# Modulation with its weight blocks stationary, in a two-layer trunk step on one core

## The chip, the cores and the metric

The kernel runs on one core of one Trainium2 chip. The metric is device time in microseconds of one execution. Three runs of the kernel before are shown; their median is the time before.

## What is computed

Two layers of a diffusion trunk, for 512 latent tokens and 128 context tokens of width 1024, all in fp32. Every layer is:

```
m = silu(c) @ w_mod[L] + b_mod[L]        # 6 vectors of 1024: shift, scale, gate, twice
h = rms_norm(x) * scale + shift          # latent tokens take c, context tokens c_ctx
x = x + gate * mixer(h)                  # layer 0: chunk gating + grouped attention; layer 1: MLA + short conv
h = rms_norm(x) * scale2 + shift2
logits = h @ w_router; aff = softmax(logits over the 16 experts)
gate, idx = top_k(aff, capacity)         # 64 latent and 16 context tokens for each expert
y[idx] += gate * (silu(h[idx] @ w_gate) * (h[idx] @ w_up)) @ w_down
x = x + gate2 * y
```

w_mod is 2 x 1024 x 6144 fp32, 48 MB. It is used for two vectors alone, c and c_ctx.

## The kernel before

**Streams.** All large weights (w_mod, the projections, 16 experts of 6 MB a layer) come in pieces of 1 MB through four `stage` slots, 128 partitions x 2048. SyncE (SP) issues them in the order of `plan_weights`; a piece is issued once the slot's last reader is done (`load`, L612 on, for the experts `expert_piece`, L629 on). Projection and expert weights are split in two parts: ScalarE (ACT) copies the high one into one of three w_hi slots (L1355, L1635), VectorE (DVE) subtracts for the low one (w_lo, L1740), and TensorE (PE) makes three passes. All of PE's products are issued in helper L800, its transposes at their own lines.

**Order of the work.** Each engine's program is written out by hand. Layer: norm sums on PE (`arena,cst`, a matrix of constants), root and scaling on DVE and ACT, projections, attention, output projection, norm sums again, then the eight tiles of h with the router's products (`logits`, 48 products with `router_hi`/`router_lo`), softmax, transposes of the affinities (L1216), transposes of h (L1224, 40 of them) which ACT copies out and sends to `h_dram`, the top-k on DVE (L2091 to L2098), the gates' transposes on PE (L1243, L1244), their copies by ACT into `gates` and `slots` (L1644 to L1649). With the slots there, GpSimd (POOL) gathers each expert's 80 rows from `h_dram` by an indirect transfer (L766), four ahead; PE transposes them (L1258), and at an expert's end POOL adds the rows to `acc_dram` by an indirect transfer (L775). At the start of layer 1 the sum is read back (`arena<-acc_dram`).

**The modulation.** It is 24 chunks of 512 columns of w_mod, 12 for each layer, two pieces of 1 MB for each chunk. The table `MOD_AT` (L98) says at which named place of the program each chunk lies, and the PSUM plan (`PsumPlan`, L109 on), the weight stream and all engines follow it. For a chunk (`mod_rows`, L865) silu(c) and silu(c_ctx) are the stationary operand, padded to 32 columns (`sP`), and w_mod moves:

```
ins = mm(bank(("mod rows", c))[32 * k:32 * k + 32, :], sP[:, 4 * half + k, :], w[:, k, :], half == 0, half == 1)
```

Eight such products of 512 columns leave the result as rows, in four strips of a bank. ACT copies the bank to `mrow` (L1342), PE turns it with four transposes (`turn_mod`, L873, L877), and DVE adds the four strips (L1826), adds the bias (L1829) and for two chunks of a layer makes `amul` (L1834). `sel` (a selection matrix) later shares `mrow`'s space.

Of the kernel before, what the change touches and what calls it, by code (L numbers as in the profile page):

```python
# [28 lines left out]
P = 128  # L29
D = 1024  # L30
# [62 lines left out]
def turned_banks(i):  # L93
# [4 lines left out]
MOD_AT = {"start": [0, 1, 2, 3], "qk": [4, 5], "first scores": [6, 7], (0, "out"): [8, 9], (0, "norm"): [], (0, "apply"): [10, 11], (0, "soft"): [],  # L98
          (0, "top"): [12, 13, 14], "acc": [15, 16], "next norm": [17], "cq": [18, 19], (1, "out"): [20, 21], (1, "norm"): [],
          (1, "apply"): [22, 23], (1, "soft"): [], (1, "top"): []}  # L100
# [6 lines left out]
class PsumPlan:  # L107
# [21 lines left out]
    def one(self, name, reader, banks=1):  # L129

        b = self.ring % 8
        if banks == 2:
            b = (b + b % 2) % 8
        self.add(name, list(range(b, b + banks)), reader)
        self.ring = b + banks
# [13 lines left out]
def plan_psum():  # L149
# [3 lines left out]
    def mod(at):  # L153

        chunks = MOD_AT[at]
        for n, c in enumerate(chunks):
            one(("mod rows", c), "act")
            if n:
                one(("mod turned", c - 1), "dve")
        if chunks:  # L160
            one(("mod turned", chunks[-1]), "dve")
# [5 lines left out]
    for c in MOD_AT["start"]:  # L167
        one(("mod rows", c), "act")
        if c == 2:
            one(("mod turned", 1), "dve")  # L170
        elif c:
            one(("mod turned", c - 1), "dve")
        if c == 1:
            one((0, "norm", 0), "dve", 2)
    one(("mod turned", MOD_AT["start"][-1]), "dve")
    for L in range(LAYERS):
# [51 lines left out]
        for n in range(len(STEPS) + LAG[L] + 1):  # L228
            if n < len(STEPS):
                p.add((L, "S", n), [0, 1, 2, 3], "act")  # L230
            if L == 0 and 1 <= n <= len(MOD_AT["first scores"]):
                p.add(("mod turned", MOD_AT["first scores"][n - 1]), [2 * n + 3], "dve")
            if L == 0 and n < len(MOD_AT["first scores"]):
                p.add(("mod rows", MOD_AT["first scores"][n]), [2 * n + 4], "act")
# [6 lines left out]
        for m in range(KD):  # L241
            p.add((L, "out", m), [2 * (m % 3), 2 * (m % 3) + 1], "dve")
        p.add((L, "norm", 1), [6, 7], "dve")
        p.ring = 0
        mod((L, "out")), mod((L, "norm")), mod((L, "apply"))
        one((L, "logits"), "act", 2)
        one((L, "logits turned"), "dve")
        mod((L, "soft"))
        one((L, "aff"), "act"), one((L, "aff ctx"), "act")
        for t in range(NT):  # L250
            one((L, "h", t), "act", 2)
        if L == LAYERS - 1:
            one("gate rows", "act")
            for t in range(NT):
                one(("x out", t), "act", 2)
        mod((L, "top"))
# [1975 lines left out]
```

## Time and profile before

| | before |
|---|---|
| median of 3 runs | 1506.52 us (1504.7 to 1508.73) |
| profiled execution | 1508.51 us, of which the span of its instructions is 1506.6 |
| PE busy | 1275.3 us (85%) |
| DVE busy | 888.4 us (59%) |
| ACT busy | 736.9 us (49%) |
| POOL busy | 226.8 us (15%) |
| granted clock of PE, mean | 0.924 of 2.4 GHz |
| moved | 323.19 MB, 215 GB/s over the span |

Times in the trace count from the span's start. The experts of layer 0 run from about 421 to 733, those of layer 1 from about 1163 to 1480. "PEld" is PE's weight load, which can overlap the product before it. An fp32 product appears as two records.

### The profile page before, as it was taken

The page shows a single profiled execution, that of the slowest core. Times are in us where ns is not written, and L with a number is a line of the kernel's source. Part 1 is how long each engine was busy: PE and PEld are TensorE (multiplying, and loading weights), DVE is VectorE, ACT ScalarE, POOL GpSimd, SP SyncE. Part 2 cuts the span into 40 slices and gives each one's busy share as a digit, 9 for nine tenths or more (in the row PEclk, how much of TensorE's full clock was granted, in tenths as well). Part 3 has the DMA queues.
Part 4 walks back from the last instruction along what each step waited for, and adds up shares of the span by engine and source line. Part 5 has one row for each costly group of instructions (what it writes and reads, how often), then busy time and mean ns, then how long its engine had stood idle before and what let it go on. Part 6 is the DMA issues. An engine that isn't in the chain of part 4 may idle for free.

```text
span 1506.6 us, 18070 instructions
## 1 busy us (share of the span) xinstructions
PE 1275.3 (85%) x7500; PEld 921.2 (61%) x7500; DVE 888.4 (59%) x989; ACT 736.9 (49%) x867; POOL 226.8 (15%) x129
## 2 busy tenths in 40 slices
PE   5899968997489988989659998999964999998991
PEld 3779736893256555556449984668933655555560
DVE  3612476325758778878374252553156878887883
ACT  2512247414447777767253114553144765666662
POOL 3000010020102222211050000000101023333230
PEclk9889889997689999999789998899976999999996
DMA  9702071006779999999872320003058799999985
GB/s 342 220 29 84 28 279 47 1 29 223 292 242 344 359 355 355 364 357 360 270 216 85 98 87 28 1 2 112 1 223 290 279 355 322 357 360 338 358 321 166
DMA packets 99047, 323.19 MB, mean 215 GB/s; under 512 B 6367, under 2 KB 30142, under 8 KB 82582
## 3 DMA queue, kind: packets, MB, share of 16 engines
q1 hardware_dynamic: 87360, 283.54, 52.3%
q0 software_dynamic: 9152, 30.53, 8.0%
q10 hardware_dynamic: 2454, 7.96, 1.4%
q8 instruction: 60, 0.98, 0.3%
q14 instruction: 21, 0.17, 0.0%
HBM read 298.20 MB, written 23.81 MB: 214 GB/s over the span
## 4 chain that ended last, share of the span: by engine, by line
PE 45%; DMA 23%; DVE 15%; ACT 13%; issue 3%; POOL 1%; ACTq 0%; SPq 0%; DVEq 0%; POOLq 0%
PE psum L800 42%; DMA stage<-in_moe_w_up 9%; DVE w_lo L1740 8%; ACT w_hi L1635 5%; DMA stage<-in_moe_w_gate 4%; ACT arena L1562 3%; DMA stage<-in_moe_w_down 2%; DMA stage<-in_w_mod 2%; DMA acc_dram<-arena 2%; DVE arena L2010 2%; DMA arena<-h_dram,arena 1%; ACT arena L1342 1%; POOL arena L684 1%; DMA arena<-acc_dram 1%; DVE h_lo L1740 1%
## 5 line engine op out<-in xcount | busy, mean ns | idle before, releaser
L1740 DVE TENSOR_TENSOR w_lo<-stage,w_hi 128x2048 fp32r<-128x2048 f32 (+1 forms) x216 | 490.4, 2280 | 222.1 <-ACT w_hi L1635 123.7
L1635 ACT ACTIVATE w_hi<-stage 128x2048 fp32r<-128x2048 f32 x192 | 366.6, 1914 | 154.9 <-DMA stage<-in_moe_w_up 49.4
L800 PE MATMUL psum<-w_hi,h_hi 128*80 128x512 f32 (+1 forms) x848 | 333.6, 393 | 55.0 <-DVE w_lo L1740 39.6
L800 PE MATMUL psum<-w_lo,h_hi 128*80 128x512 f32 (+1 forms) x848 | 328.1, 387 | 0.0
L800 PE MATMUL psum<-w_hi,h_lo 128*80 128x512 f32 (+1 forms) x848 | 327.5, 386 | 0.0
L800 PE MATMUL psum<-h_hi,w_hi 128*128 128x320 f32 x672 | 211.3, 314 | 4.7 <-DVE h_lo L1784 4.7
L800 PEld LDWEIGHTS psum<-w_hi,h_hi 128*80 128x80 f32 (+1 forms) x848 | 130.9, 154 | 136.7 <-DVE w_lo L1740 42.3
L800 PE MATMUL psum<-h_lo,w_hi 128*128 128x320 f32 x672 | 209.8, 312 | 0.0
L800 PE MATMUL psum<-h_hi,w_lo 128*128 128x320 f32 x672 | 209.6, 312 | 0.0
L775 POOL DMA_INDIRECT acc_dram<-arena x32 | 101.1, 3160 | 482.4 <-ACT arena L1673 252.7
L800 PEld LDWEIGHTS psum<-w_hi,h_lo 128*80 128x80 f32 (+1 forms) x848 | 131.1, 155 | 64.4 <-issue 2.5
L800 PEld LDWEIGHTS psum<-w_lo,h_hi 128*80 128x80 f32 (+1 forms) x848 | 131.3, 155 | 53.8 <-issue 1.9
L800 PE MATMUL psum<-arena 128*64 128x128 f32 (+8 forms) x940 | 132.5, 388 | 24.4 <-ACT arena L1562 10.2
L1342 ACT ACTIVATE arena<-psum 128x256 f32<-128x256 f32 (+7 forms) x133 | 75.3, 615 | 137.1 <-PE psum L800 120.0
L800 PEld LDWEIGHTS psum<-h_hi,w_hi 128*128 128x128 f32 x672 | 128.2, 191 | 6.4 <-issue 6.4
L800 PEld LDWEIGHTS psum<-h_lo,w_hi 128*128 128x128 f32 x672 | 128.2, 191 | 0.2 <-issue 0.2
L800 PEld LDWEIGHTS psum<-h_hi,w_lo 128*128 128x128 f32 x672 | 128.1, 191 | 0.0
L800 PEld LDWEIGHTS psum<-arena 128*64 128x64 f32 (+4 forms) x940 | 78.0, 175 | 81.1 <-issue 55.7
L1562 ACT ACTIVATE arena<-psum,arena 128x640 f32<-128x640 f32 x64 | 50.3, 790 | 63.8 <-DVE arena L2010 63.8
L684 POOL TENSOR_TENSOR arena<-arena 128x640 f32<-128x640 f32 x24 | 39.0, 1626 | 272.7 <-ACT arena L1365 271.2
L1355 ACT ACTIVATE w_hi<-stage 128x2048 fp32r<-128x2048 f32 x22 | 41.9, 1910 | 66.9 <-PE psum L800 63.4
L1365 ACT ACTIVATE arena<-xT 128x640 f32<-128x640 f32 x32 | 23.1, 735 | 100.7 <-DVE xT L2068 73.1
(225 smaller groups left out, 1200.5 us busy)
## 6 DMA issues: line engine op xcount, KB each, us to landing
stage<-in_moe_w_gate SPq DMA_DIRECT2D x64, 1024.0 KB, 8.5
stage<-in_moe_w_up SPq DMA_DIRECT2D x64, 1024.0 KB, 8.9
stage<-in_moe_w_down SPq DMA_DIRECT2D x64, 1024.0 KB, 7.3
stage<-in_w_mod SPq DMA_DIRECT2D x48, 1024.0 KB, 7.8
stage<-in_ev_w_in SPq DMA_DIRECT2D x7, 1024.0 KB, 10.8
stage<-in_od_w_in SPq DMA_DIRECT2D x7, 1024.0 KB, 10.0
h_dram<-arena ACTq DMA_DIRECT2D x10, 512.0 KB, 3.4
stage<-in_ev_w_out SPq DMA_DIRECT2D x4, 1024.0 KB, 5.4
```

The lines of the kernel that those rows point to most:

```text
L684: nc.gpsimd.tensor_tensor(rstd, rstd, sq[k % 2], ALU.add).then_inc(sq_added, 1)
L775: pool.indirect_dma_start(acc_dram[L], bass.IndirectOffsetOnAxis(slots[:, e:e + 1], 0), ysb[e % 2], None, compute_op=ALU.add).then_inc(sca ...
L800: return pe.matmul(o, w, x, start=first, stop=last, skip_group_check=True)
L1342: freeing(nc.scalar.activation(dst, src, ACT.Copy, **kw))
L1355: nc.scalar.activation(split_slot(w_hi, pc["q"], pc["n"]), slot(pc), ACT.Copy).then_inc(hi_ready, 1)
L1365: nc.scalar.activation(rstd if k == 0 else sq[k % 2], xT[:, k, :], ACT.Square).then_inc(sq_ready, 1)
L1562: ins = nc.scalar.activation(p[:, LKEYS * a:LKEYS * a + LKEYS], src[:, 0:LKEYS], ACT.Exp, bias=largest(i, a), accum_out=total(i, a))
L1635: nc.scalar.activation(split_slot(w_hi, q0), stage[:, PIECE * (p0 % SLOTS):PIECE * (p0 % SLOTS) + PIECE], ACT.Copy)\
L1740: return nc.vector.tensor_tensor(dst, src, hi.bitcast(F32), ALU.subtract)
L2010: ins = nc.vector.tensor_reduce(largest(i, a), src[:, 0:LKEYS], AX.X, ALU.max, negate=True)
```

## The change

The weight block becomes the stationary operand. A chunk is 32 products: 128x128 of w_mod stationary, the two columns of `sT` (silu(c), silu(c_ctx)) moving. The result falls out with features on partitions, so `sP`, `mrow`, the ACT copy, the transposes and the DVE reduction go; DVE adds the bias from the bank (`turned_mod`). A chunk can be issued in eight parts (`mod_part`).

The chunks' places change. (0, out), (0, apply) and (0, top) with 2, 2 and 3 chunks become: 8 ahead of the norm sums ("sum"), 9 and 10 behind them ("root"), 11 in eight parts among the logits' products, 12 ahead of the transposes of h ("rank"), 13 between the context's gates and the latent gates ("top"), and 14 moves to the end of the layer ("acc"). In layer 1: 20 ahead of the norm sums, 21 and 22 behind, 23 among the logits. DVE takes up the results at these places, some of them before the top-k and some behind the slots.

Around the top-k: DVE, not ACT, copies the latent gates and slots out, right behind the top-k; ACT first copies the context's, then splits g0, g1 and u0 of expert 0; DVE splits the first gathered rows ahead of u0. SP holds the fifth expert piece until the first gather has landed. POOL issues the gate rows' transfers behind the first four gathers, and `final_norm` goes to `cs`, issued earlier. The banks of the PSUM plan around it are fixed by number.

```diff
...
-          (1, "apply"): [22, 23], (1, "soft"): [], (1, "top"): []}
+MOD_AT = {"start": [0, 1, 2, 3], "qk": [4, 5], "first scores": [6, 7], (0, "sum"): [8], (0, "root"): [9, 10], (0, "logits"): [11],
+          (0, "rank"): [12], (0, "top"): [13], "acc": [14, 15, 16], "next norm": [17], "cq": [18, 19], (1, "sum"): [20],
+          (1, "root"): [21, 22], (1, "logits"): [23], (1, "rank"): [], (1, "top"): []}
...
                     else:
+                        if m == SLOTS:
+                            sp.wait_ge(gathered[0], 16 * (E // AHEAD * L + 1))
                         sp.wait_ge(lo_ready, m + (moe_q[L] - SLOTS + 1))
...
+            def mod_part(c, i):
+
+                name, (half, k) = ("mod", c), divmod(i, 4)
+                pc = piece[("mod", c, half)]
+                if i == 0:
+                    begin(name)
+                if k == 0:
                     pe.wait_ge(stage_in[pc["p"] % SLOTS], arrived(pc["p"]))
-                    for k in range(4):
-                        ins = mm(bank(("mod rows", c))[32 * k:32 * k + 32, :], sP[:, 4 * half + k, :], w[:, k, :], half == 0, half == 1)
+                w = slot(pc).rearrange("p (k n) -> p k n", k=4)
+                for b in range(MODC // P):
+                    ins = mm(bank(name)[:, 2 * b:2 * b + 2], w[:, k, P * b:P * b + P], sT[:, i, :], i == 0 and b == 0, i == KD - 1)
+                if k == 3:
                     ins.then_inc(psum_full if half else mod_used, 1)
...
-            for c in MOD_AT["start"]:
-                mod_rows(c)
-                if c:
-                    turn_mod(c - 1)
-                if c == 1:
-                    norm_sum_of_two((0, "norm", 0))
-            turn_mod(MOD_AT["start"][-1])
+            modulation("start", slice(0, 2))
+            norm_sum_of_two((0, "norm", 0))
+            modulation("start", slice(2, None))
...
+                modulation((L, "sum"))
                 norm_sum_of_two((L, "norm", 1))
-                modulation((L, "out"))
-                modulation((L, "norm"))
-                modulation((L, "apply"))
+                modulation((L, "root"))
...
                 for k in range(KD):
+                    for c in MOD_AT[(L, "logits")]:
+                        mod_part(c, k)
                     h_tile(h0 + KD + k + 1)
...
-                for what in ("g0", "g1", "u0")[:2 + L]:
-                    expert_split(0, what)
...
-                filled(act, (L, "gates"))
-                src = bank((L, "gates"))[0:CAP_L, :]
-                nc.scalar.activation(gates[0:CAP_L, :], src[:, 0:E], ACT.Copy)
-                freeing(nc.scalar.activation(slots[0:CAP_L, :], src[:, E:2 * E], ACT.Copy))
-                if L == 0:
-                    expert_split(0, "u0")
+                for what in ("g0", "g1", "u0"):
+                    expert_split(0, what)
...
-                groups = bank(name).rearrange("p (b k r) -> p b r k", b=nb, k=4)[:, :, 0:2, :]
-                freeing(nc.vector.tensor_reduce(new, groups, AX.X, ALU.add))
+                bias = bcol[:, nb * c:nb * c + nb].rearrange("p (b o) -> p b o", o=1).to_broadcast([P, nb, 2])
+                freeing(nc.vector.tensor_tensor(new, bank(name)[:, 0:2 * nb].rearrange("p (b g) -> p b g", g=2), bias, ALU.add))
...
                 nc.vector.tensor_copy(idxf[0:E, :], idx[0:E, :]).then_inc(topk_done, 1)
+                filled(dve, (L, "gates"))
+                if L == 0:
+                    dve.wait_ge(new_out, 32)
+                src = bank((L, "gates"))[0:CAP_L, :]
+                nc.vector.tensor_copy(gates[0:CAP_L, :], src[:, 0:E])
+                freeing(nc.vector.tensor_copy(slots[0:CAP_L, :], src[:, E:2 * E]))
+                modulation((L, "rank"))
                 modulation((L, "top"))
...
-                for what in ("g0", "g1", "u0"):
-                    expert_split(0, what)
+                expert_split(0, "g0")
+                expert_split(0, "g1")
                 rows_split(0)
+                expert_split(0, "u0")
```

What moves on PE at the start of layer 0, from the transposes of x (L850, after L854) to the first projection (`w_hi,h_hi`); `arena,cst` are the norm sums. Before:

```order
L850 MATMUL psum<-cst,arena 128x128 x32
L800 MATMUL psum<-stage,sP 32x512 x16
L877 MATMUL psum<-cst,mrow 128x128 x4
L800 MATMUL psum<-arena,cst 128x512
L800 MATMUL psum<-arena,cst 128x128
L800 MATMUL psum<-arena,cst 128x512
L800 MATMUL psum<-arena,cst 128x128
L800 MATMUL psum<-stage,sP 32x512 x8
L877 MATMUL psum<-cst,mrow 128x128 x4
L800 MATMUL psum<-stage,sP 32x512 x8
L877 MATMUL psum<-cst,mrow 128x128 x8
```

And after the change:

```order
L854 MATMUL psum<-cst,arena 128x128 x32
L804 MATMUL psum<-sT,stage 128x2 x64
L804 MATMUL psum<-arena,cst 128x512
L804 MATMUL psum<-arena,cst 128x128
L804 MATMUL psum<-arena,cst 128x512
L804 MATMUL psum<-arena,cst 128x128
L804 MATMUL psum<-sT,stage 128x2 x64
L804 MATMUL psum<-w_hi,h_hi 128x256
```

The places stay; 16 products and 8 transposes for two chunks become 64 products with two columns.

On PE behind the output projection of layer 0, from the norm sums to the first router products. Before:

```order
L800 MATMUL psum<-arena,cst 128x512
L800 MATMUL psum<-arena,cst 128x128
L800 MATMUL psum<-stage,sP 32x512 x16
L877 MATMUL psum<-cst,mrow 128x128 x8
L800 MATMUL psum<-stage,sP 32x512 x16
L877 MATMUL psum<-cst,mrow 128x128 x8
L800 MATMUL psum<-h_hi,router_hi 16x320
```

After, from the end of the output projection:

```order
L804 MATMUL psum<-sT,stage 128x2 x32
L804 MATMUL psum<-arena,cst 128x512
L804 MATMUL psum<-arena,cst 128x128
L804 MATMUL psum<-arena,cst 128x512
L804 MATMUL psum<-arena,cst 128x128
L804 MATMUL psum<-sT,stage 128x2 x68
L804 MATMUL psum<-h_hi,router_hi 16x320
```

One chunk now stands ahead of the norm sums, two and the first part of a fourth behind them; its other seven parts follow among the router's products.

On PE from the affinities' transposes (L1216, after L1209) to the first gathered rows (L1258, after L1252). Before:

```order
L1216 MATMUL psum<-cst,arena 16x128 x4
L800 MATMUL psum<-cst,arena 16x128
L1224 MATMUL psum<-cst,arena 128x128 x40
L800 MATMUL psum<-stage,sP 32x512 x16
L877 MATMUL psum<-cst,mrow 128x128 x4
L800 MATMUL psum<-stage,sP 32x512 x8
L877 MATMUL psum<-cst,mrow 128x128 x8
L800 MATMUL psum<-cst,arena 16x16 x2
L1243 MATMUL psum<-cst,arena 64x16
L1244 MATMUL psum<-cst,arena 64x16
L1258 MATMUL psum<-cst,arena 128x80 x8
```

After:

```order
L1209 MATMUL psum<-cst,arena 16x128 x4
L804 MATMUL psum<-cst,arena 16x128
L804 MATMUL psum<-sT,stage 128x2 x32
L1218 MATMUL psum<-cst,arena 128x128 x40
L804 MATMUL psum<-cst,arena 16x16 x2
L804 MATMUL psum<-sT,stage 128x2 x32
L1237 MATMUL psum<-cst,arena 64x16
L1238 MATMUL psum<-cst,arena 64x16
L1252 MATMUL psum<-cst,arena 128x80 x8
```

Three chunks ahead of both gates become one ahead of the transposes of h and one between the two gates.

## Rows read from the trace of the kernel before

**Rows 1.** The page: busy time of the engines, granted clock in 40 slices (tenths).

```profile
PE 1275.3 (85%) x7500; PEld 921.2 (61%) x7500; DVE 888.4 (59%) x989; ACT 736.9 (49%) x867; POOL 226.8 (15%) x129
...
PEclk9889889997689999999789998899976999999996
```

**Rows 2.** The page: the chain that ended last, shares by engine.

```profile
PE 45%; DMA 23%; DVE 15%; ACT 13%; issue 3%; POOL 1%; ACTq 0%; SPq 0%; DVEq 0%; POOLq 0%
```

**Rows 3.** Windows: length, busy us (count) of PE, PEld, DVE, ACT, POOL; clock, DMA share, GB/s.

```profile
436.00:733.00 297.00, 273.69 (x1284) 173.95 (x1288) 232.58 (x138) 208.97 (x153) 56.33 (x26) 0.99 1.00 353
1180.00:1470.00 290.00, 269.32 (x1249) 171.23 (x1247) 241.97 (x148) 188.75 (x134) 83.36 (x25) 0.99 0.97 341
```

**Rows 4.** Timeline, two chunks of modulation in layer 0: start, duration, engine.

```profile
344.56 3.64 PE L800 MATMUL psum<-stage,sP 128*32 128x512 f32 x32
...
348.13 0.66 PE L877 MATMUL psum<-cst,mrow 128*128 128x128 f32 x4
```

**Rows 5.** Timeline, weight loads: norm sums warm, cold, short transposes; last, the group's mean.

```profile
343.28 0.30 PEld L800 LDWEIGHTS psum<-arena,cst 128*128 128x128 f32 x2 [1.17 <-ACT arena L1365]
...
343.82 0.19 PEld L800 LDWEIGHTS psum<-arena,cst 128*128 128x128 f32 x1 [0.24 <-issue]
...
27.42 0.55 PEld L800 LDWEIGHTS psum<-arena,cst 128*128 128x128 f32 x2
...
28.48 0.33 PEld L800 LDWEIGHTS psum<-arena,cst 128*128 128x128 f32 x1 [0.52 <-issue]
...
377.46 0.39 PEld L1210 LDWEIGHTS psum<-cst,arena 16*128 16x128 f32 x5 [1.14 <-ACT arena L1342]
...
L800 PEld LDWEIGHTS psum<-arena,cst 128*128 128x128 f32 x60 | 11.5, 212 | 20.3 <-issue 17.4 <-ACT arena L1365 2.3 <-DVE arena L1892 0.2
```

**Rows 6.** Windows at changes of the clock, columns as in rows 3.

```profile
29.60:39.80 10.20, 6.19 (x46) 2.31 (x45) 3.95 (x7) 4.37 (x5) 2.69 (x3) 1.00 0.95 294
...
78.90:84.20 5.30, 5.30 (x40) 2.68 (x42) 3.49 (x3) 1.72 (x1) 0.00 (x0) 1.00 0.03 5
84.20:95.20 11.00, 11.00 (x58) 6.63 (x58) 1.38 (x2) 0.00 (x0) 0.00 (x0) 0.50 0.28 94
...
1127.70:1132.00 4.30, 4.30 (x22) 4.30 (x22) 3.67 (x9) 2.04 (x4) 0.00 (x0) 0.50 0.12 44
1132.00:1135.40 3.40, 3.40 (x31) 3.19 (x31) 3.20 (x9) 2.46 (x3) 0.00 (x0) 0.99 0.84 336
```

**Rows 7.** The chain at the start: start, duration, what.

```profile
46.11 13.96 PE psum L800 x100
```

**Rows 8.** The chain at the first scores of layer 0.

```profile
201.50 2.09 PE psum L800 x16
...
207.43 1.37 PE psum L800 x8
...
211.40 1.37 PE psum L800 x8
```

**Rows 9.** The chain from the second norm of layer 0 to its first gather.

```profile
376.72 0.70 ACT arena L1342
...
404.66 0.16 PE psum L1243
...
407.69 10.52 DMA arena<-h_dram,arena
```

**Rows 10.** The chain at the end: the last scatter.

```profile
1480.14 5.12 DMA acc_dram<-arena
```

**Rows 11.** The chain at the start of layer 1.

```profile
748.28 1.13 PE psum L845 x4
```

**Rows 12.** The chain at cq, layer 1.

```profile
902.30 9.94 PE psum L800 x35
```

**Rows 13.** The chain at the first gather of layer 1.

```profile
1146.89 3.69 ACT w_hi L1635 x2
...
1151.40 8.33 DMA arena<-h_dram,arena
```

More of the change, by code:

```diff
@@ L133, in one @@
             b = (b + b % 2) % 8
-        self.add(name, list(range(b, b + banks)), reader)
+        self.add(name, list(range(b, b + banks)), reader, in_order)
         self.ring = b + banks
@@ L153, in mod @@
     def mod(at):
[L155 to L161, printed above, removed]
+        for c in MOD_AT[at]:
+            one(("mod", c), "dve")
     one("cols", "act"), one("bias cols", "act")
@@ L167, in plan_psum @@
     for c in MOD_AT["start"]:
[L168 to L172, printed above, removed]
+        one(("mod", c), "dve")
         if c == 1:
             one((0, "norm", 0), "dve", 2)
-    one(("mod turned", MOD_AT["start"][-1]), "dve")
     for L in range(LAYERS):
@@ L230, in plan_psum @@
                 p.add((L, "S", n), [0, 1, 2, 3], "act")
-            if L == 0 and 1 <= n <= len(MOD_AT["first scores"]):
-                p.add(("mod turned", MOD_AT["first scores"][n - 1]), [2 * n + 3], "dve")
             if L == 0 and n < len(MOD_AT["first scores"]):
-                p.add(("mod rows", MOD_AT["first scores"][n]), [2 * n + 4], "act")
+                p.add(("mod", MOD_AT["first scores"][n]), [2 * n + 4], "dve")
             if 0 <= n - LAG[L] < len(STEPS):
@@ L311, in plan_weights @@
             out(2), out(3)
-        mod((L, "out")), mod((L, "norm")), mod((L, "apply")), mod((L, "soft")), mod((L, "top"))
+        mod((L, "sum")), mod((L, "root")), mod((L, "logits")), mod((L, "rank")), mod((L, "top"))
         for m in range(6 * E):
@@ L779, in _ @@
                     gather(e)
+                if L == LAYERS - 1:
+                    emptied(pool, ("x out", NT - 1))
+                    pool.wait_ge(gate_turned_out, 16)
+                    for rows, g in ((slice(0, CAP_L), 0), (slice(CAP_L, CAP), 1)):
+                        pool.dma_start(gate_rows[rows, :].rearrange("q (k p) -> q k p", k=KD),
+                                       gate_dram[:, g, :].rearrange("(o k) p -> o k p", o=1).to_broadcast([rows.stop - rows.start, KD, P]))\
+                            .then_inc(gate_rows_in, 16)
                 for e in range(E):
@@ L1174, in _ @@
                         scores(n)
[L1175 to L1176 removed]
                     if L == 0 and n < len(MOD_AT["first scores"]):
[L1178 removed]
+                        mod_chunk(MOD_AT["first scores"][n])
                     if 0 <= n - LAG[L] < len(STEPS):
@@ L1234, in _ @@
                         ins.then_inc(psum_full, 1)
-                modulation((L, "top"))
                 pe.wait_ge(ranked_ctx, L + 1)
@@ L1240, in _ @@
                 mm(bank((L, "gates ctx"))[CAP_L:CAP, E:2 * E], idxf[CTX_ROW:RANKED, 0:CAP_C], both, True, True).then_inc(psum_full, 1)
+                modulation((L, "top"))
                 pe.wait_ge(topk_done, L + 1)
@@ L1441, in _ @@
                     root_of(L, 0)
-                    modulation("next norm")
                 shifted(L, 0)
@@ L1590, in _ @@
                         exponent(n)
-                    if L == 0 and n < len(MOD_AT["first scores"]):
-                        modulation("first scores", slice(n, n + 1))
                     if 0 <= n - LAG[L] < len(STEPS):
@@ L1599, in _ @@
                 root_of(L, 1)
-                modulation((L, "out"))
-                modulation((L, "norm"))
                 shifted(L, 1)
@@ L1626, in _ @@
                         act.dma_start(acc_dram[L][P * t:P * t + P, :], x_out[t]).then_inc(x_stored, 16)
-                modulation((L, "top"))
                 n0 = E * L
@@ L1766, in norm @@
             def norm(L, which):
+                if which == 1:
+                    modulation((L, "sum"))
                 if (L, which) != (0, 0):
                     root_of((L, "norm", which))
+                if which == 1:
+                    modulation((L, "root"), slice(0, 1))
                 def scaled(k):
@@ L1789, in norm @@
                     return
-                modulation((L, "out"))
-                modulation((L, "norm"))
                 for k in range(KD + 2):
@@ L1840, in modulation @@
                     turned_mod(c)
-            then(nc.vector.memset(sP_[:, :], 0.0))
             dve.wait_ge(consts_in, 16)
@@ L2084, in _ @@
                     .then_inc(aff_done, 1)
+                modulation((L, "root"), slice(1, None))
+                modulation((L, "logits"))
                 emptied(dve, (L, "aff ctx"))
```

122 lines of the change are left out of this document (45 added, 77 removed).

## The prediction

> **What bounds the kernel now.** I read the page from the top. TensorE (PE) is busy 85% of the span, more than any other engine, and the row of granted clock stands near full speed nearly everywhere, with dips in the slices between the long stages, where the modulation is computed [rows 1]. The chain that ended last gives PE 45% and transfers 23% [rows 2]. So I went from shares to stretches. While the experts run, the transfer engines are at 1.00 and 0.97 and move 353 and 341 GB/s, PE at full clock beside them [rows 3]: the expert stretches (about 590 of 1506.6 us) are bound by their weights, and nothing in the change alters them. The question is the other 900 us, where the 24 chunks of modulation lie. There PE runs from one product to the next, and a chunk is work on PE in the gap between two stages.
>
> **One chunk, before and after.** Before, two chunks are 32 matmul records of 512 columns in 3.64 us, so 1.8 us each, and then 0.66 us of transposes, with an ACT copy between [rows 4]. After, a chunk is 32 fp32 products, each with a 128-column block of w_mod as stationary operand and 2 columns moving. The 16 records of a chunk before were 8 fp32 products, so each fp32 product is two weight loads: 64 loads per chunk. With 2 columns to stream, the loads are the price. The trace has fp32 loads of 128 columns in the norm sums. Two in a row take 0.30 us where one takes 0.19, and in a stretch at low clock 0.55 against 0.33 [rows 5]: the next starts 0.11 or 0.22 us behind the first. That is 256 cycles at 2.4 GHz and at 1.2 GHz (0.107 and 0.213 us). So a chunk costs 64 x 0.107 = **6.8 us warm** and 64 x 0.213 = **13.7 us cold**. The other bound is the short loads ahead of transposes: five start within 0.39 us, with the last 0.14 long, so 0.063 us apart [rows 5], and a chunk would be 64 x 0.063 = 4.0 us. I take the first pair, since it is the same instruction form (a true fp32 operand, split in two loads), and keep 4.0 for the range.
>
> The Trainium skill ("TensorE: Matmul & The Clock Gate", section on LDWEIGHTS) gives a load as the column count over 1.2, in ns: 107 for 128 columns, whatever the clock. The warm rows agree with it, the cold ones don't. By its figure every chunk would cost 6.8 us, even with the clock at its lower level.
>
> **Which clock.** 78.9 to 84.2 PE is busy for all of 5.30 us at clock 1.00, then 84.2 to 95.2 busy for all of 11.00 us at 0.50 [rows 6]. The products there have a stationary operand of 8 rows. So a PE that never idles can lose its clock. Through the long expert stretches, full 128-row products with 512 columns, it stays at 0.99 [rows 3]. The new stream is nearly only loads, with 2 columns moved for each pair of them; of the stretches that the trace has, it resembles the 8-row one most. The forecast is that about 4 us into a stream of chunks the clock falls, so that n chunks in a row cost 13.7n - 4 us. Against this stand the transposes from 1127.7 on, begun at 0.50 and at 0.99 from 1132 on [rows 6], though they stream 128 columns each. So this is a forecast with a rival beside it.
>
> **The places, cold.** "Before" is the time of the row named.
> 1. Start: PE takes up chunk 0 at 18.3. Chunks 0 and 1 cost 23.4, the norm sums 3.3, chunks 2 and 3 27.4, and from the last product to the first projection 3.9 us passed before (42.2 to 46.11). 18.3 + 23.4 + 3.3 + 27.4 + 3.9 = 76.3 against 46.11 [rows 7]: +30.2. The weights that wait for chunk 2's slot come later as well, but are hidden by chunk 3.
> 2. q/k and first scores: chunks 4, 5 from 188.28: 23.4 -> 211.7, where the first scores ran at 201.50; then scores 2.1 and chunk 6 at 13.7 -> 227.5 against 207.43; then 1.4 and chunk 7 -> 242.6 against 211.40 [rows 8]: +31.2.
> 3. Layer 0 to the first gather. Chunk 8 now lies ahead of the norm sums (+9.7), chunks 9 and 10 (27.4) lie where PE waited for w_mod, and the eight parts of chunk 11 lie among 48 router products (13.7 + 12.7). 341.1 + 9.7 + 3.3 + 27.4 + 26.4 = 407.9 against 376.7 [rows 9]: +31.2. The whole chain to the ranking moves with it. Chunk 12 (13.7) now lies ahead of the 40 transposes of h and chunk 13 ahead of the gates: 411.9 + 13.7 + 6.2 + 10 to 13 = 443, against 404.66: +38. Then what the change gives back: latent slots no longer wait behind a 1.90 us split on ACT (404.97 to 407.69, some 2.5 us), and the first gather runs without the weights beside it. It took 10.52 us; the nearest transfer of its sort with nothing beside it is the last scatter, 5.12 [rows 9, 10]. So -5.4 at most. The hold has a price: the fifth weight piece is issued after the gather lands. Before it left at 407.50, and the experts' stream is what bounds them, so of the 8 us won some 3 are lost. Sum +38 - 2.5 - 5.4 + 3 = +33.
> 4. Before the second layer: chunks 14, 15, 16 from 733: 37.1 -> 770, while the sum of layer 0 came at 748.28 [rows 11]: +21.8. Chunk 17 lies behind the norm sums: +4.
> 5. cq: chunks 18, 19 from 896.46, 23.4 -> 919.9 against 902.3 [rows 12]: +17.6.
> 6. Layer 1 to the gather: like place 3, without chunks 12 and 13: +31.2. Back: the gates were made at 1146.3, but ACT's splits ran until 1150.6 and the gather was issued at 1151.40, and landed 8.33 later [rows 13]: -4.5 and -3.2, less some 3 for the hold: +26.5.
>
> Sum: 30.2 + 31.2 + 33 + 21.8 + 4 + 17.6 + 26.5 = 164. In three places the norm sums stand between chunks, and before they brought the clock back (loads of 0.33 us at 28.48 [rows 5], clock 1.00 from 29.6 [rows 6]); about 3 us each, -10. **+154 on 1508.5: 1662, or 1660 beside the median**, which is 2.0 below the profiled time.
>
> Costed at nothing: the bias add on VectorE instead of reduce and add, sP's memset, final_norm's earlier load (POOL idle there), gate_rows behind four gathers (needed only at the end, over 300 us later), and the ACT copies gone; at each of these places PE is last by far. If the chunks prove cheap these come into play for under 1 us each.
>
> **Rivals.**
> A. **The clock stays.** The loads count as work and the stretch behaves as the transposes did. Then 6.8 us a chunk: start 18.3 + 13.7 + 3.3 + 13.7 + 3.9 = 52.9, +6.8; scores +7.8; layer 0 logits end at 341.1 + 6.8 + 2.6 + 13.7 + 7.1 + 6.8 = 378.1, +1.4, and the top-k (399.26) not PE sets the gates: 401.7 against 404.7, so -3.0, then -2.7, -5.4 and +3: -8; place 4 +5.2; place 5 +8; layer 1 +0.3 - 4.5 - 3.2 + 2.5 = -5. Sum +15: 1522. For it: long warm rows everywhere else. Against: the 8-row stretch. The skill's figure for a load gives this same time with either clock.
> B. **Loads are as short as those of transposes**, and the change is faster. 4.0 us a chunk, warm: places 1 and 2 then hide behind the weights (va's piece, 37.5) and behind the rotation that ends at 201.5: 0; place 3 -12, place 6 -9, place 4 +2, place 5 +2. That is -17, and up to -28 if the hold costs nothing: 1480 to 1490. It decides below about 5 us a chunk. For it: the 0.063 us of other loads. Against: 60 fp32 loads of this very shape take 212 ns in the mean, where those short ones took 137 [rows 5].
> C. **It cancels.** Chunks of 5 to 6 us, the added 1 to 5 us of each place returned by the two gathers: 1502 to 1511.
>
> **How the numbers follow.** Forecast (cold) 0.48, A 0.24, B 0.20, C 0.08. The likeliest case's own range is 1620 to 1690 (the clock coming back more often, or none of the give-backs). With A and the nearer end of B the range is **1482 to 1688**. About 0.3%, 4.5 us, is what this kernel's measurement can tell from no change. Faster: B, 0.20; same: C, 0.08; slower: the forecast and A, 0.72. The time is the likeliest case's, 1660.
>
> **What would show it.** The windows of the chunks: right if PE is busy throughout at clock 0.50 with loads 0.33 long and 32 products in 13 to 14 us; the first projection near 76, the gather of layer 0 issued near 445 and landing within 6 us. Wrong if the clock stays at 1.00 there (A), if the chunks take under 5 us (B), or if the gather still takes 10 us with no weights beside it.

## The result and the profile after

The changed kernel takes 1666.08 us in the median of 4 runs (1662.36 to 1673.12), the kernel before 1506.01 on the same chips (1504.7 to 1508.73, 4 runs): the ratio is 1.107, with a 95% interval of 1.102 to 1.111. The profiled execution of the changed kernel is its slowest, 1673.12 us with a span of 1671.3, so 164.6 us above the profiled one of before where the medians lie 160.1 apart.

The page of the changed kernel, its busy times, granted clock and chain, in place of [rows 1, 2]:

```profile
span 1671.3 us, 20087 instructions
...
PE 1519.0 (91%) x8556; PEld 1204.4 (72%) x8556; DVE 883.3 (53%) x968; ACT 723.7 (43%) x839; POOL 225.6 (13%) x129
...
PEclk7589866998557999999956997899985799999996
...
PE 59%; DMA 18%; DVE 11%; ACT 9%; issue 2%; POOL 1%; ACTq 0%; SPq 0%; POOLq 0%; DVEq 0%
```

PE is busy 244 us more, the mean of its clock went from 0.924 to 0.86, and the chain gives PE 59% where it gave 45%. VectorE and ScalarE did get rid of their work (DVE 888.4 to 883.3, ACT 736.9 to 723.7), and nothing came of it. The lowest digits of the clock's row (5 and 6) lie in slices 2, 6 and 7, 11 and 12, 21 and 22, and 31, where chunks lie; the 6 of the last slice stood in the row of before as well.

The groups of the new products, from the same page (line, engine, operation, count, busy us, mean ns):

```profile
L804 PEld LDWEIGHTS psum<-sT,stage 128*128 128x128 f32 x1536 | 300.0, 304 | 4.6 <-ACT arena L1640 1.7
L804 PE MATMUL psum<-sT,stage 128*128 128x2 f32 x1536 | 297.4, 330 | 1.2 <-ACT arena L1640 1.2
```

1536 records for 768 products: an fp32 product is two loads and two passes, as assumed. The mean load is 304 ns, nearer the 0.33 of the cold row than the 0.19 of the warm one [rows 5]. What a chunk costs stands in the windows over them (length, busy us and count of PE, PEld, DVE, ACT, POOL; clock, DMA share, GB/s):

```profile
18.30:22.80 4.50, 4.50 (x42) 4.50 (x41) 1.86 (x4) 2.21 (x3) 4.07 (x4) 0.99 0.70 254
22.80:41.00 18.20, 18.20 (x87) 18.20 (x87) 0.17 (x1) 1.47 (x2) 3.71 (x3) 0.50 0.54 173
45.50:72.50 27.00, 27.00 (x129) 27.00 (x128) 5.66 (x6) 3.38 (x3) 2.69 (x3) 0.50 0.49 143
218.90:224.00 5.10, 5.10 (x49) 5.10 (x47) 5.10 (x1) 0.59 (x1) 5.10 (x2) 1.00 0.13 18
259.30:272.80 13.50, 13.50 (x66) 13.50 (x64) 2.95 (x6) 1.66 (x4) 0.00 (x0) 0.50 0.40 133
418.80:422.00 3.20, 3.20 (x29) 3.02 (x28) 0.95 (x2) 1.47 (x2) 0.00 (x0) 1.00 0.34 132
422.20:445.00 22.80, 22.80 (x109) 22.80 (x109) 15.01 (x29) 12.52 (x24) 0.00 (x0) 0.50 0.43 139
1244.70:1248.10 3.40, 3.40 (x33) 3.40 (x32) 1.50 (x2) 1.47 (x2) 0.00 (x0) 1.00 0.10 34
1248.30:1270.00 21.70, 21.70 (x103) 21.70 (x103) 14.37 (x28) 12.40 (x24) 0.00 (x0) 0.50 0.45 146
```

The stretch that begins at 18.3 keeps its clock for the first 4.5 us, the one at 218.9 for 5.1; chunk 8, from 405.0 on, keeps it until 408.4, some 3.5 us. After that it stands at 0.50 with PE busy throughout, and 64 loads (259.3 to 272.8, chunk 7) fill 13.50 us: 0.21 us each, against the 13.7 of the forecast. Behind the norm sums of layer 0, at 418.8, and of layer 1, at 1244.7, the clock is back for some 3.3 us and falls again.

The chain of waits at the places of the prediction. First the start and the scores (start, duration, what):

```profile
18.26 54.50 PE psum L804 x264
...
76.59 3.54 PE psum L804 x15
```

The first projection is at 76.59, 30.5 us later than at 46.11 [rows 7] (forecast: 76.3). From chunk 0 on the chain is PE alone. Then layer 0 from the logits to the first weights behind the gather, and the same of layer 1:

```profile
469.06 0.70 ACT arena L1336
...
504.19 0.16 PE psum L1237
...
505.56 5.58 DMA arena<-h_dram,arena
...
511.53 14.75 DMA stage<-in_moe_w_gate
...
1294.19 0.70 ACT arena L1336
...
1317.68 0.23 PE psum L1237
...
1319.07 5.52 DMA arena<-h_dram,arena
...
1324.98 14.37 DMA stage<-in_moe_w_gate
```

The last row of the logits is copied at 469.06 where it was at 376.72 [rows 9], +92.3. The gather is issued at 505.56 and takes 5.58 us in place of 10.52. In layer 1 it is issued at 1319.07 and takes 5.52 in place of 8.33 [rows 13]. Both times the chain then goes over the held weights: the fifth piece is issued as the gather lands (511.15 and 1324.61), and the one behind it, on the chain, is 14.75 and 14.37 us on the way.

Set against before, by the first instruction of each place in the two timelines. The last column is the prediction's sum for that place, without its -10 for a clock that comes back:

| place | before | after | later by | added since the row above | forecast for it |
|---|---|---|---|---|---|
| first projection, layer 0 | 46.1 | 76.6 | 30.5 | 30.5 | 30.2 |
| logits of layer 0 copied | 376.7 | 469.1 | 92.3 | 61.8 | 62.4 |
| first gathered rows turned | 418.3 | 511.2 | 92.9 | 0.6 | -1 |
| rows of the third expert turned | 448.0 | 544.1 | 96.1 | 3.1 | +3 (hold) |
| last expert's rows, layer 0 | 697.5 | 794.7 | 97.1 | 1.1 | 0 |
| sum of layer 0 on PE | 748.3 | 868.7 | 120.4 | 23.3 | 21.8 |
| behind cq's chunks | 902.3 | 1044.9 | 142.6 | 22.2 | 4 + 17.6 |
| logits of layer 1 copied | 1123.1 | 1294.2 | 171.1 | 28.5 | 31.2 |
| first gathered rows turned | 1159.8 | 1324.7 | 164.9 | -6.3 | -7.7 |
| end | 1506.6 | 1671.3 | 164.7 | -0.2 | +3 (hold) |

### The profile page after: what moved, and what is told of

Read it like the earlier page. It is cut to its first block, busy times and chain, and to the rows that moved or that the text cites. A ratio compares the mean times of both kernels' runs of the same rounds, so it can differ in the third digit from the quotient of the medians.

```text
span 1671.3 us, 20087 instructions
## 1 busy us (share of the span) xinstructions
PE 1519.0 (91%) x8556; PEld 1204.4 (72%) x8556; DVE 883.3 (53%) x968; ACT 723.7 (43%) x839; POOL 225.6 (13%) x129
## 4 chain that ended last, share of the span: by engine, by line
PE 59%; DMA 18%; DVE 11%; ACT 9%; issue 2%; POOL 1%; ACTq 0%; SPq 0%; POOLq 0%; DVEq 0%
PE psum L804 57%; DVE w_lo L1705 7%; DMA stage<-in_moe_w_up 6%; DMA stage<-in_moe_w_gate 5%; DMA stage<-in_moe_w_down 4%; ACT w_hi L1608 4%; ACT arena L1541 3%; DVE arena L1971 2%; DMA acc_dram<-arena 1%; DMA arena<-h_dram,arena 1%; POOL arena L686 1%; ACT arena L1336 1%; DVE h_lo L1705 0%; ACT arena L1640 0%; DVE arena L2150 0%
## 5 line engine op out<-in xcount | busy, mean ns | idle before, releaser
L1608 ACT ACTIVATE w_hi<-stage 128x2048 fp32r<-128x2048 f32 x192 | 366.7, 1914 | 162.4 <-DMA stage<-in_moe_w_up 50.2
L804 PEld LDWEIGHTS psum<-sT,stage 128*128 128x128 f32 x1536 | 300.0, 304 | 4.6 <-ACT arena L1640 1.7
L804 PE MATMUL psum<-sT,stage 128*128 128x2 f32 x1536 | 297.4, 330 | 1.2 <-ACT arena L1640 1.2
L772 POOL DMA_INDIRECT acc_dram<-arena x32 | 94.2, 2943 | 486.8 <-ACT arena L1640 256.0
L804 PE MATMUL psum<-arena 128*64 128x128 f32 (+8 forms) x940 | 137.1, 396 | 15.2 <-ACT arena L1541 8.8
```

Of the source, the lines that this page charges most:

```text
L772: pool.indirect_dma_start(acc_dram[L], bass.IndirectOffsetOnAxis(slots[:, e:e + 1], 0), ysb[e % 2], None, compute_op=ALU.add).then_inc(sca ...
L804: return pe.matmul(o, w, x, start=first, stop=last, skip_group_check=True)
L1608: nc.scalar.activation(split_slot(w_hi, q0), stage[:, PIECE * (p0 % SLOTS):PIECE * (p0 % SLOTS) + PIECE], ACT.Copy)\
```

## The experiments

The kernel before was timed beside each group of runs: 1505.72 us (18 runs), 1507.09 (17) and 1508.26 (15). It varied more there than in the three runs shown, from 1494.73 to 1515.84. So each run below is compared by its ratio.

### 128 columns moving in place of 2

```diff
-                    ins = mm(bank(name)[:, 2 * b:2 * b + 2], w[:, k, P * b:P * b + P], sT[:, i, :], i == 0 and b == 0, i == KD - 1)
+                    ins = mm(bank(name)[:, P * b:P * b + 128].rearrange("p (r g) -> p r g", g=2), w[:, k, P * b:P * b + P],
+                             sT[:, i:i + 1, :].to_broadcast([P, 64, 2]), i == 0 and b == 0, i == KD - 1)
...
-bank(name)[:, 0:2 * nb].rearrange("p (b g) -> p b g", g=2), bias
+bank(name).rearrange("p (b g) -> p b g", b=nb)[:, :, 0:2], bias
```

> The changed kernel, but each modulation product moves 128 columns (the two columns of sT, repeated 64 times) instead of 2, with the same 64 weight loads per chunk. Theory 1: the clock fell because these products move almost no columns. Then PE stays at its full clock through the chunks, the 1536 loads take about 0.19 us and not 0.30 in the mean, and a chunk costs between 6.8 us (64 x 0.107, the columns stream while the next load runs) and 13.7 us (load and columns in turn). Total between about 1522 us and the changed kernel's 1666: the same or faster, though 64 times the columns are moved. Theory 2: the loads themselves let the clock fall, whatever moves. Then the clock is 0.50 in the chunks as now, a chunk costs at least 13.7 us and up to 27, and the total is 1666 to 1900 us.

1526.73 us (1518.6 to 1536.28, 4 runs), ratio to before 1.015 (1.010 to 1.021), mean clock 0.959. This is 139 us below the changed kernel, with the same loads and 64 times the columns. Its windows over the same chunks, and the group of its loads:

```profile
17.60:31.80 14.20, 14.20 (x130) 14.20 (x128) 2.69 (x6) 3.69 (x5) 8.43 (x6) 1.00 0.86 286
34.10:48.30 14.20, 14.20 (x129) 14.20 (x128) 5.67 (x6) 3.38 (x3) 2.69 (x3) 1.00 0.82 254
188.10:202.30 14.20, 14.20 (x129) 14.20 (x128) 12.23 (x13) 0.75 (x1) 6.16 (x3) 1.00 0.62 197
...
L804 PEld LDWEIGHTS psum<-sT,stage 128*128 128x128 f32 x1536 | 174.3, 191 | 3.8 <-ACT arena L1641 1.7 <-DMA stage<-in_w_mod 0.4 <-DVE arena L1883 0.3
```

The clock is 1.00 in every chunk. 128 loads fill 14.20 us, so a chunk is 7.1 us, or 0.111 us a load: the columns cost next to nothing beside the loads, 4% more than the 0.107 that the loads alone were to take. The first projection came at 52.4 where rival A had worked out 52.9, and the total within 5 us of rival A's 1522: its prices hold once the clock stays up. Theory 2 is out: the same loads do not lower the clock when 128 columns move behind each. The number of loads, the places and the program's waits are unchanged, so what the 139 us bought back is the clock, in the chunks and in the work right behind them.

### 32 columns

The same edit with 32 columns (`[P, 16, 2]`).

> As the run with 128 columns, but 32 columns. Theory 1: between the two others; the columns themselves are hidden under any load (0.027 us at full clock against 0.107), so if the clock stays up the total is near 1522 us, and if it does not it is the changed kernel's 1666. Theory 2: 1666 us, clock 0.50 in the chunks.

1660.16 us (1658.07 to 1668.23, 4 runs), ratio 1.103 (1.097 to 1.108), mean clock 0.867. Its windows:

```profile
18.80:23.60 4.80, 4.80 (x46) 4.80 (x44) 1.84 (x4) 2.21 (x3) 4.36 (x4) 1.00 0.63 227
23.80:41.40 17.60, 17.60 (x85) 17.60 (x84) 0.17 (x1) 1.48 (x2) 3.20 (x3) 0.50 0.53 177
237.50:250.90 13.40, 13.40 (x65) 13.40 (x64) 2.18 (x4) 2.90 (x16) 0.00 (x0) 0.50 0.42 149
```

The clock goes the way that it went with 2 columns: 1.00 for the first 4.8 us, then 0.50, and 13.40 us for 64 loads. The loads are the same in number at 2, 32 and 128 columns; of the three widths only 128 kept the clock. What lies between was not run, and no rule is drawn from three widths.

### The form alone, at the places of before

In the kernel before, the chunks became 32 products with the block stationary. `MOD_AT` stayed, slots were copied by ScalarE, nothing was held.

```diff
-                        ins = mm(bank(("mod rows", c))[32 * k:32 * k + 32, :], sP[:, 4 * half + k, :], w[:, k, :], half == 0, half == 1)
+                        for b in range(MODC // P):
+                            ins = mm(bank(("mod turned", c))[:, 2 * b:2 * b + 2], w[:, k, P * b:P * b + P], sT[:, 4 * half + k, :],
+                                     half == 0 and k == 0 and b == 0, half == 1 and k == 3)
...
-                groups = bank(name).rearrange("p (b k r) -> p b r k", b=nb, k=4)[:, :, 0:2, :]
-                freeing(nc.vector.tensor_reduce(new, groups, AX.X, ALU.add))
```

> The kernel before with the form of the modulation alone changed: 32 products with the w_mod block stationary and 2 columns moving, at the places of before; slots on ScalarE and no hold, as before. Theory 1 (the price is the chunk's weight loads at the lower clock, wherever it stands): every chunk costs 13 to 14 us in place of 2.5; layer 0 has one more chunk ahead of its gates than the whole change has, and the gathers are not made earlier, so 1666 plus 10 to 20 us: 1675 to 1690. Rival (the new places are what costs, since PE waits there for w_mod and everything behind waits for PE): well below 1666, under 1600.

1671.44 us (1670.58 to 1675.28, 4 runs), ratio 1.110 (1.105 to 1.116). So the form alone makes the whole loss, and the rival (the places) is out. It is 4 us less than the lower end of what was expected. In its timeline the first gathered rows of layer 0 come at 525.5, 14.3 us behind the changed kernel's 511.2, as the third chunk ahead of the gates would have it; but it has one chunk less at the end of the layer, and at the logits of layer 1 it is 4 us ahead. A chunk moved from one place with PE on the path to another such place costs about the same there.

### The form alone, with 128 columns

The kernel above with the edit of the first experiment.

> As the run before, with 128 columns moving (the two of sT repeated 64 times). Theory 1 (128 columns keep PE's clock up): chunks at 7.2 us as in the earlier run with 128 columns, clock 1.00 there, and the total some 140 us below the form alone, 1530 to 1545; above the earlier run with 128 columns (1527), by what the places and the earlier gathers are worth. Theory 2 (that run's gain came from its places): clock 0.50 in the chunks, above 1650.

1539.4 us (1538.7 to 1540.95, 4 runs), ratio 1.022 (1.017 to 1.027), mean clock 0.957: 132 us below the form alone, in the bounds given. The clock stays up at the old places too. Both pairs put the rest of the change (new places, slots by VectorE, the hold) on the side of a gain: 5 us between the medians with 2 columns (1671.44 to 1666.08), some 12 us with 128 (1539.4 to 1526.73, ratio 1.022 to 1.015). In both pairs the intervals overlap, so its size is not settled here.

### Slots by VectorE, and the hold, with the modulation of before

```diff
+                filled(dve, (L, "gates"))
+                if L == 0:
+                    dve.wait_ge(new_out, 32)
+                src = bank((L, "gates"))[0:CAP_L, :]
+                nc.vector.tensor_copy(gates[0:CAP_L, :], src[:, 0:E])
+                freeing(nc.vector.tensor_copy(slots[0:CAP_L, :], src[:, E:2 * E]))
```

with ScalarE's copies of the latent gates and slots gone and its three splits behind those of the context (run "evict"). In the second run ("evict_hold") also SP's wait on `gathered[0]` and VectorE's order g0, g1, rows, u0, both as in the change.

> The kernel before with one part of the change: VectorE copies the latent gates and slots out behind the top-k, ScalarE copies the context's first and then splits. No hold, modulation as before. Theory 1 (the gather waits for ScalarE's splits and nothing else): layer 0's first gather is issued 2.5 us earlier, layer 1's 4.5 us earlier, each still taking 8 to 10 us beside the weights, and the total falls by 4 to 7 us, to about 1500. Theory 2 (the expert stretch is bound by its weights, so an earlier gather only waits elsewhere): gathers earlier, total within 2 us of 1506.

> The run before, and in addition SyncE holds the fifth expert piece until the first gather has landed and VectorE splits the first rows ahead of the third piece: the whole part of the change that is not modulation. Theory 1: each first gather takes 5.5 us in place of 10.5 and 8.3, but the held piece costs some 3 us of the weight stream in each layer, so another 2 us or less off the run without the hold: 1496 to 1500. Rival: the hold costs as much as it saves, no difference from the run without it (1500), or the stream is so much later that it is slower, 1504 to 1510.

The eviction alone: 1499.92 us (12 runs), ratio 0.9967 (0.9939 to 0.9995). With the hold: 1492.63 us (7 runs), ratio 0.9910 (0.9873 to 0.9947). A repeat in the last group gave 1494.54 (10 runs) and 0.9910 (0.9879 to 0.9940). The gathers in the two chains, of "evict" at 405.12 and 1137.26:

```profile
405.12 5.81 DMA arena<-h_dram,arena
...
1137.26 15.75 DMA arena<-h_dram,arena
```

and of "evict_hold":

```profile
407.05 6.51 DMA arena<-h_dram,arena
...
1139.34 7.20 DMA arena<-h_dram,arena
```

From the affinities' transposes (L1216 before) to the rows turned, by the timelines:

| | before | evict | evict_hold | changed kernel | changed, no hold |
|---|---|---|---|---|---|
| layer 0, first rows | 38.5 | 31.5 | 31.9 | 38.8 | 42.0 |
| layer 0, third expert's rows | 68.2 | 61.4 | 61.4 | 71.7 | 72.6 |
| layer 1, first rows | 33.7 | 36.9 | 28.3 | 27.2 | 30.3 |
| layer 1, third expert's rows | 63.0 | 67.9 | 58.7 | 58.0 | 59.6 |

In layer 0 the eviction gives 7 us, more than the 2.5 by which the gather was issued earlier: issued at 405.12, 3.2 us ahead of the next weight pieces (408.31), it has landed in 5.81 us, where before the pieces left at 407.50 and the gather at 407.69. In layer 1 it is issued earlier as well but two weight pieces follow 1.4 us behind it (from 1138.68); it takes 15.75 us and loses 3 us against before. With the hold it takes 7.20 us, and the third expert's rows come 9 us earlier than without. In neither layer did the hold lengthen the way to the third expert here.

Two things keep this from being a clean test of the hold. The second run also changed VectorE's order around the first rows. And both runs lack a part of the change: POOL still issues `final_norm` (512 KB) and the gate rows some 4 us ahead of layer 1's gather, at 1133.15 and 1133.69 in "evict", where the changed kernel has them elsewhere and its gather takes 5.52 us. So "evict_hold" is not quite all that the change has beside its modulation, and which of these transfers made the 15.75 us was not taken apart. The eviction came out as theory 1 had it in its total, but not in where it comes from: layer 1 lost by it. The second step is worth 7 us between the medians, more than the 2 expected; the intervals of the two ratios (0.9939 to 0.9995 and 0.9873 to 0.9947) overlap by a little.

### The changed kernel without its hold

```diff
-                        if m == SLOTS:
-                            sp.wait_ge(gathered[0], 16 * (E // AHEAD * L + 1))
```

> The changed kernel without the hold on the fifth expert piece. In its trace the first gather took 5.6 us in both layers, and from the first gathered rows to the third expert's 32.8 us in layer 0 and 30.9 in layer 1, where before it was 29.7 and 29.3. Theory 1 (the hold costs some 3 us of the weight stream and saves the gather its company): without it the gathers take 8 to 16 us again and those stretches shrink to about 30; the two nearly cancel, total within 5 us of 1666. Rival (the hold is what makes the whole change slow in part): 1655 or less. Rival (the gather's gain is real and the hold's price is not): 1672 or more.

1669.12 us (1666.26 to 1673.79, 4 runs), ratio 1.110 (1.105 to 1.115), beside the changed kernel's 1.107 (1.102 to 1.111): the intervals overlap, and no worth of the hold can be told here. Its gathers took longer:

```profile
508.17 8.70 DMA arena<-h_dram,arena
...
1313.04 8.61 DMA arena<-h_dram,arena
```

8.70 and 8.61 us instead of 5.58 and 5.52. By the table the hold brings the first rows 3 us earlier in each layer, and of this 1 to 1.5 us are left at the third expert: from the first rows to the third expert's it is 30.6 and 29.3 us without the hold, 32.8 and 30.9 with it, so here the hold has a price of some 2 us and returns 3. Nor does the hold alone make a gather short: in the run with 128 columns, which has it, layer 0's gather took 9.43 us, issued 1.9 us behind an earlier weight piece (412.56).

### A better order for the kernel before

"evict" and "evict_hold" leave the row form of the modulation (2.5 us a chunk) with two other parts of the change. Three waits for w_mod stood in the chain of before, ahead of the logits and of the gates of layer 0 and ahead of the logits of layer 1:

```profile
348.26 10.78 DMA stage<-in_w_mod
...
388.87 10.75 DMA stage<-in_w_mod
...
1093.76 10.71 DMA stage<-in_w_mod
```

Three runs took them out of the way in steps, all on "evict_hold":

```diff
-(0, "apply"): [10, 11], (0, "soft"): [], (0, "top"): [12, 13, 14], "acc": [15, 16]
+(0, "apply"): [], (0, "soft"): [10, 11], (0, "top"): [12, 13], "acc": [14, 15, 16]
...
-(1, "apply"): [22, 23], (1, "soft"): []
+(1, "apply"): [], (1, "soft"): [22, 23]
```

"acc14" has only chunk 14 moved, "soft22" also 22 and 23, "soft10" all of it.

> The run evict_hold (modulation as before, slots by VectorE, weights held), and chunk 14 moved from ahead of layer 0's gates to the end of the layer. In the chain before, the gates waited 10.75 us for w_mod (388.87) and were made at 404.7, although the top-k was there at 399.3. Theory 1: the gates come some 4 to 5 us earlier, the 2 MB are no longer read there, and the chunk's 2.5 us at the end of the layer lie beside the reading of the sum (733 to 748): 1487 to 1489 against evict_hold's 1492.6. Rival: the chunk's pieces delay the reading of the sum at the layer's end by as much, since both are transfers: no difference.

> As acc14, and chunks 22 and 23 of layer 1 moved from ahead of the logits (where the chain waited 10.71 us for w_mod at 1093.76) to behind their transposes, beside the softmax. Theory 1: the logits of layer 1 end up to 8 us earlier, the two chunks (5 us) cover 2.4 us of softmax and delay the affinities by the rest: 3 to 5 us less than acc14. Rival: the router's products are paced by the eight tiles of h (1.66 us each), not by w_mod, and the softmax now waits for the chunks: 3 us more.

> As soft22, and in layer 0 likewise chunks 10 and 11 moved from ahead of the logits to behind their transposes. In the trace of soft22 the chain still waits 10.70 us for w_mod at 347.95 in layer 0; in layer 1, where the same move was made, the affinities came 4.2 us earlier than in acc14. Theory: the same 3 to 5 us in layer 0, total 1487 to 1489 where soft22 has 1491.8. Rival: the order of the expert pieces behind these chunks in the stream makes expert 0's weights later by the same, no difference.

| | median | runs | ratio to before | 95% |
|---|---|---|---|---|
| evict_hold, twice | 1492.63, 1494.54 | 7, 10 | 0.991, 0.991 | 0.987 to 0.995, 0.988 to 0.994 |
| acc14 | 1493.74 | 12 | 0.992 | 0.989 to 0.995 |
| soft22 | 1491.82 | 6 | 0.990 | 0.985 to 0.994 |
| soft10 | 1485.97 | 6 | 0.988 | 0.985 to 0.992 |

"acc14" missed its 4 to 5 us. From the affinities of layer 0 to the first rows it takes 28.9 us, where evict_hold has 31.9 and its repeat 31.4: the move gives 2.5 to 3 us there, and the total shows nothing of it that its spread would let one see. "soft22" has its layer 1 affinities 4.2 us earlier than "acc14" by the timelines, of which 1.1 were there in layer 0 already; the total again hardly moved (2 us for 3 to 5). "soft10" is the lowest, a little under its forecast of 1487 to 1489 and 8.6 us below the evict_hold of its own group, though the two intervals overlap. Its chain in layer 0:

```profile
360.63 1.94 PE psum L803 x12
...
362.59 0.70 ACT arena L1345
...
372.37 5.80 PE psum L1227 x40
...
381.18 11.90 DMA h_dram<-arena
...
394.02 6.13 DMA arena<-h_dram,arena
```

The logits are copied at 362.59 where before had 376.72, but 4.5 us of these 14 are not the order's: a piece of the chain that is the same in both, the 432 records of PE from the stretch of [rows 6] on, took 62.51 us in this execution and 67.06 in that of before, where the clock fell earlier. The gather then waits for h's tiles to be written (11.90 us, from 381.18): the next bound there is this transfer. These ratios lie close together; what they carry is that all four are below before. soft10 has the lowest median of the study, and how much of that is its order is not shown.

## Why the prediction held

**The price of a chunk.** Forecast 13.7 us cold, from loads 0.213 us apart; measured 13.50 us for 64 loads at clock 0.50. The warm price, 6.8, was measured by the 128-column run at 7.1. Rival B's short loads (0.063 us) did not occur at either clock. They were loads for transposes of 16 rows.

**The clock.** The forecast took the step from one stretch in which PE never idled and lost its clock all the same (78.9 to 95.2, [rows 6]). The step came true, in the chunks (0.50) and in the total, but the likeness that it rests on is not what made it so, and in this there is luck. What decides in the chunks is shown by the pair of runs that differ in moved columns alone: 1.00 in every chunk with 128, 0.50 with 2 and 32. The stretch that the forecast took as its nearest moved 512 and 128 columns a product, and only some of its products had a stationary operand of 8 rows; the others, between them, had 128 rows and 64 columns. Its first products in the timeline of before:

```profile
78.87 1.12 PE L800 MATMUL psum<-small,mrow 8*128 8x512 f32 x2 [0.60 <-ACT arena L1342]
79.92 1.09 PE L800 MATMUL psum<-arena 128*64 128x128 f32 x16
```

Nor is it a steady example. The same products, read at their place in all 13 traces of this case, lost the clock within 6 us in ten of them, kept it for 11 us at least in two (the 128-column run and "soft10") and for all of 16.3 us in one, the form alone with 128 columns, where they begin at 85.32:

```profile
90.62:96.32 5.70, 5.70 (x54) 3.66 (x54) 1.38 (x2) 0.00 (x0) 0.00 (x0) 1.00 0.53 179
96.32:101.62 5.30, 5.30 (x39) 5.07 (x38) 0.69 (x1) 0.00 (x0) 0.00 (x0) 1.00 0.00 0
```

Why the clock fell there in the kernel before stays open. The transposes, which spoke for rival A, moved 128 columns each; the 128-column run shows that they were the wrong comparison for a product with 2. The 4 us for which the clock was to stay at the head of a row of chunks stand in no row (the stretch of [rows 6] kept it for at least 5.30 us); the runs show 4.5, 5.1 and some 3.5.

The Trainium skill ("TensorE: Matmul & The Clock Gate", section on LDWEIGHTS) gives one time for a load of 128 columns, 107 ns, with no term for the clock. The changed kernel's loads are 0.21 us apart at 0.50 and the 128-column run's 0.111 at 1.00, so here it held at the higher level only.

**Places 1 to 5.** Each came within 2 us: +30.5 against +30.2; +61.8 against +62.4 for places 2 and 3 to the logits; +23.3 against +21.8; +22.2 against +21.6 for chunk 17 and cq. **Place 6**: +28.5 against +31.2, and the give-back of the gather 6.3 against 7.7. The sign "gather of layer 0 issued near 445" counted place 3 alone; with the 61 us of places 1 and 2 before it, it is 504 to 506, and it was issued at 505.56.

**The gather and the hold.** A gather with no weights beside it was put at 5.1 us by the last scatter, and the two are 5.6 and 5.5 (in layer 0 with the piece u1 issued 1.3 us ahead of it, at 504.22). In layer 0 the 3 us that the hold was to cost did appear (3.1 between the first rows and the third expert's). Without the hold 2.2 of them are gone (30.6 us for this stretch against 32.8), but the first rows come 3.2 later, so that the way from the affinities to the third expert's rows is no shorter (72.6 against 71.7 us); and evict_hold has the hold and no such price (29.5 us for the stretch, 29.7 before). So the price hangs on what else is under way. In layer 1 it was 1.6 us at the third expert's rows and gone at the end (-0.2), where the sum had +3. What the rest of layer 0's 3 us is, is open. In its timeline u1, the fourth piece of expert 0, is issued at 504.22 only, when chunk 13 has left its slots; that this is the reason was argued, not tried.

**The term that was mis-sized** is the -10 for a clock that comes back behind the norm sums. At the start it did not come back at all (0.50 over all of 45.5 to 72.5, beyond the sums), and in each layer's second norm it was back for 3.3 us, which is worth as much: some 6 or 7 us, and those are in the rows of the table already. Without the term the sum was 164, and the profiled execution is 164.6 above its counterpart. That the two agree to 1 us is luck: row by row the forecast was off by up to 3 us, some 6.5 us in all too low and as much too high. With the term the forecast was 1660, 6 us below the median.

**How sure it was.** The forecast had a chance of 0.48, and the stated range, 1482 to 1688, takes in a faster kernel as well as a slower one; that the time lies in it says little. What carries weight is the likeliest case, 1660 against 1666.08, with the prices and delays above.

**Costed at nothing** held as far as it can be seen. The removed work on ScalarE (24 copies of 0.6 us) and VectorE bought nothing that the totals show; on the chain from chunk 0 to the first projection there is PE alone.

## What to carry to other kernels

A product with a 128x128 fp32 block stationary and a few columns moving costs its loads, here 64 for a chunk (13.5 us at the lower clock, 7.1 at the higher); the alternative, 512 columns streamed past a small stationary operand, took 2.5 us with its transposes. Before making a weight stationary to save copies and transposes on other engines, count loads and look whether those engines are ever last. If such a stream is unavoidable, watch the granted clock, not the busy share: PE read 100% busy in the slow stretches and in the fast ones, and repeating two columns 64 times made the same kernel 139 us faster. It was still slower than the kernel before, 1526.73 against 1505.72. And take a bundle apart: with the modulation of before, the eviction and the hold are worth 13 us (1492.63 against 1505.72), and in this bundle they lay under a loss of 160.

## What the runs showed that was not expected

- More moved columns, less time: 1526.73 us with 128 columns, where 2 took 1666.08 and 32 took 1660.16, these two within each other's intervals (1.102 to 1.111 and 1.097 to 1.108).
- With the slots copied by VectorE and no hold, the first gather took 5.81 us in layer 0 and 15.75 in layer 1, beside the weight pieces, where before it was 10.52 and 8.33. In these four gathers an earlier issue did not by itself mean an earlier landing.
- The kernel before varied from 1494.73 to 1515.84 us over 50 runs on these chips, five times as widely as in its first three, so gains of 5 us needed ten runs to be seen and a step of 2 us between acc14 and soft22 was not seen at all. The spread goes with PE's clock: the 12 executions below 1501 us have a mean granted clock of 0.928 to 0.935, the 10 above 1509.4 us one of 0.922 to 0.928.
- The same products at the same place (layer 0, the stretch of [rows 6]) lost the clock within 6 us in ten traces and kept it for 11 us or more in three, which alone makes 4.5 us (67.06 against 62.51).
